# Gate and queries of the attention branch as seven block products, with GpSimd adding the token sums, in a one-core hybrid retention and differential-attention step

## What is computed

```python
h = rmsnorm(x, norm1_g) * (1.0 + scale1) + shift1
proj = h @ w_in
q_r, k_r, v_r, g_r, q_d, k_d, v_d, gates = split_projection(proj)
gates = jax.nn.sigmoid(gates + b_gate)
gate_r, gate_d = jnp.split(gates, 2, axis=-1)
...  # rotary positions on q_r, k_r, q_d, k_d of the latent tokens
y_r = head_group_norm(out_f + jnp.flip(out_b_rev, 1), ret_gn_g)
branch_r = (jax.nn.silu(g_r) * y_r) @ w_ret_out
...  # differential attention of q_d over k_d, v_d and the cached keys and values
mix = (gate_r * branch_r + gate_d * branch_d) @ w_o
x = x + gate1 * mix
ffn = (jax.nn.silu(h2 @ w_ffn_gate) * (h2 @ w_ffn_up)) @ w_ffn_down
```

## Time and profile before

| | us |
|---|---|
| median of three runs | 1299.69 |
| lowest, highest | 1299.42, 1299.79 |
| the profiled execution | 1299.46 |
| its span, first to last instruction | 1297.8 |

### The profile page before, as it was taken

How to read it: one execution, slowest core, us unless ns; L and a number is a source line. 1 busy time by engine, 2 the same in 40 slices (tenths; PEclk the granted TensorE clock), 3 DMA queues, 4 the chain that set the end, 5 groups by cost and what they waited for, 6 DMA issues and landing times.

```text
span 1297.8 us, 19779 instructions
## 1 busy us (share of the span) xinstructions
PE 1259.1 (97%) x7734; PEld 1152.0 (89%) x7734; DVE 798.2 (62%) x1297; ACT 486.7 (38%) x813; POOL 300.7 (23%) x264
## 2 busy tenths in 40 slices
PE   4999999999999999999999999989999999999997
PEld 2698888899999999988788899889998999889986
DVE  4654121477657743374798844478973789557966
ACT  5452233344321122223777622245441344313434
POOL 1002000311000111110799400004510445005500
PEclk9999999999999999999999999999999999999999
DMA  9634222154434434451200234311333133222222
GB/s 309 210 98 138 65 65 82 41 157 136 129 132 130 146 98 130 114 178 50 82 2 1 82 98 146 93 38 33 98 98 97 33 97 99 97 65 66 90 89 81
DMA packets 87394, 129.59 MB, mean 100 GB/s; under 512 B 3529, under 2 KB 64450, under 8 KB 87186
## 3 DMA queue, kind: packets, MB, share of 16 engines
q1 hardware_dynamic: 77024, 95.69, 23.1%
q0 software_dynamic: 8960, 31.68, 8.1%
q10 hardware_dynamic: 1330, 1.10, 0.3%
HBM read 117.43 MB, written 4.73 MB: 94 GB/s over the span
## 4 chain that ended last, share of the span: by engine, by line
PE 90%; DVE 4%; ACT 3%; POOL 1%; issue 1%; DMA 1%; ACTq 0%; DVEq 0%
PE psum L431 31%; PE psum L468 28%; PE psum L687 18%; PE psum L1240 2%; PE psum L1224 1%; PE psum L417 1%; PE psum L1199 1%; PE psum L617 1%; PE psum L1049 1%; POOL probs L989 1%; DVE w_lo L400 1%; DMA rows<-in_diff_subln_g 1%; PE psum L1157 1%; PE psum L1197 1%; POOL probs L995 1%
## 5 line engine op out<-in xcount | busy, mean ns | idle before, releaser
L400 DVE TENSOR_TENSOR w_lo<-w_raw,w_hi 128x2048 fp32r<-128x2048 f32 x57 | 130.6, 2291 | 191.6 <-ACT w_hi L395 189.2
L395 ACT ACTIVATE w_hi<-w_raw 128x2048 fp32r<-128x2048 f32 x57 | 108.8, 1909 | 173.9 <-PE psum L468 107.8
L431 PE MATMUL psum<-h_hi,w_lo 128*128 128x320 f32 x672 | 154.7, 311 | 0.0
L431 PE MATMUL psum<-h_lo,w_hi 128*128 128x320 f32 x672 | 153.1, 309 | 0.0
L431 PE MATMUL psum<-h_hi,w_hi 128*128 128x320 f32 x672 | 153.1, 309 | 0.0
L468 PE MATMUL psum<-w_hi,hid 128*128 128x512 f32 x440 | 135.6, 389 | 0.0
L431 PEld LDWEIGHTS psum<-h_hi,w_hi 128*128 128x128 f32 x672 | 112.4, 188 | 0.0
L431 PEld LDWEIGHTS psum<-h_hi,w_lo 128*128 128x128 f32 x672 | 111.8, 188 | 0.5 <-issue 0.4
L431 PEld LDWEIGHTS psum<-h_lo,w_hi 128*128 128x128 f32 x672 | 112.2, 188 | 0.0
L687 PE MATMUL psum<-h_hi,seven_lo 128*128 128x320 f32 x320 | 98.9, 309 | 1.1 <-DVE silu_g L2296 1.1
L687 PE MATMUL psum<-h_lo,seven_hi 128*128 128x320 f32 x320 | 98.9, 309 | 0.0
(11 more groups left out here) (311 smaller groups left out, 2754.7 us busy)
## 6 DMA issues: line engine op xcount, KB each, us to landing
w_raw<-in_w_in SPq DMA_DIRECT2D x32, 1024.0 KB, 5.6
ada_b<-in_w_ada POOLq DMA_DIRECT2D x32, 512.0 KB, 4.4
w_raw<-in_w_ffn_gate SPq DMA_DIRECT2D x11, 1024.0 KB, 5.3
w_raw<-in_w_ffn_up SPq DMA_DIRECT2D x11, 1024.0 KB, 5.3
ada_a<-in_w_ada SPq DMA_DIRECT2D x8, 1024.0 KB, 13.6
w_raw<-in_w_ffn_down SPq DMA_DIRECT2D x8, 1024.0 KB, 5.1
w_raw<-in_w_ret_out SPq DMA_DIRECT2D x4, 1024.0 KB, 5.2
swapped<-qk_d POOLq DMA_DIRECT2D x32, 128.0 KB, 2.5
```

The costliest lines, as they stand in the source:

```text
L395: act.activation(w_hi[s][:, :, :], w_raw[s][:, :, :], ACT.Copy).then_inc(w_hi_done, 1)
L400: dve.tensor_tensor(w_lo[s][:, :, :], w_raw[s][:, :, :], w_hi[s][:, :, :].bitcast(F32), ALU.subtract).then_inc(w_lo_done, 1)
L431: last = pe.matmul(bank(4 * par + 2 * j + h, HALF), w[:, k, cs], x[:, k, h * HALF:(h + 1) * HALF], start=(k == 0 and n == 0), stop=(k == K ...
```

## The change

- gate_d and q_d are made by seven products of blocks, like the up phases, eight units in all; both are read out by VectorE. The order becomes gate_r, ret_out, gate_d, q_d.
- ret_out comes ahead of gate_d: the transposes of retention's output are woven into gate_r's third unit, and all four heads are normalised and gated ahead of that.
- The token block sums of h, out of high and low parts, are made by GpSimd in ten operations of 128x1280, two behind the loads of gate_r's last and each ret_out partial; ScalarE and VectorE split them.
- VectorE adds the seven products of a query unit, ScalarE scales them in place, and the rotation of unit n-1 stands in VectorE's program inside unit n of the seven units, that of (1,0) ahead of the split of the first key unit, that of (1,1) behind it.
- The adaLN partials that stood beside gate_d stand beside k_d, with buffers of their own; v_d's first stands in k_d's last rotation.
- Addresses move (gate_d, qk_d, od, v_d, the rotary table); the rows of gate1 and gate2 are loaded by two DMAs.

The diff, cut to its core (`seven_sums` is the five steps of `seven_unit`, moved to a function that both use, with the two places between them as arguments; `weight_sums` keeps its four sums, the fourth now apart as `last_weight_sum`; `B`, `Y` and so on are places in SBUF):

```diff
 PHASES = [("qk_r", 4, "act", "act"), ("v_r", 4, "act", "act"), ("g_r", 4, "act", "act"),
-          ("gate_r", 4, "act", "act"), ("gate_d", 4, "act", "act"), ("ret_out", 4, "dve", "dve"),
-          ("q_d", 4, "act", "act"), ("k_d", 4, "act", "act"), ("v_d", 4, "act", "act"),
+          ("gate_r", 4, "act", "act"), ("ret_out", 4, "dve", "dve"), ("gate_d", 4, "dve", "dve"),
+          ("q_d", 4, "dve", "dve"), ("k_d", 4, "act", "act"), ("v_d", 4, "act", "act"),
           ("diff_out", 4, "dve", "dve"), ("w_o", 4, "dve", "dve"),
...
-ADA_FIRST = {"gate_r": 0, "gate_d": 4, "ret_out": 8, "v_d": 12}
+ADA_FIRST = {"gate_r": 0, "ret_out": 4, "k_d": 8, "v_d": 12}
+SEVENS = ("gate_d", "q_d", "up0", "up1", "up2")
+GATED = ("gate_d", "q_d")
...
+        h_sum_hi = [at(f"h_sum_hi{n}", B + 5 * n, [P, KH, HALF], F32R) for n in range(4)]
+        h_sum_lo = [at(f"h_sum_lo{n}", Y + 5 * n, [P, KH, HALF], F32R) for n in range(4)]
+        h_sum = [at(f"h_sum{n}", Y + 5 * n, [P, KH, HALF]) for n in range(4)]
...
+            def token_terms():
+                hi, lo = (h_hi[:, :, :].bitcast(F32), h_lo[:, :, :].bitcast(F32))
+                x11, x21, x12, x22 = (hi[:, ks, cs] for ks in (low_k, high_k) for cs in (first_half, second_half))
+                y11, y21, y12, y22 = (lo[:, ks, cs] for ks in (low_k, high_k) for cs in (first_half, second_half))
+                z = [t[:, :, :] for t in h_sum]
+                return ((z[0], x21, x22, ALU.add), (z[0], z[0], y21, ALU.add), (z[0], z[0], y22, ALU.add),
+                        (z[1], z[0], x11, ALU.subtract), (z[1], z[1], y11, ALU.subtract),
+                        (z[3], x12, z[1], ALU.subtract), (z[3], z[3], y12, ALU.add),
+                        (z[2], x11, x21, ALU.subtract), (z[2], z[2], y11, ALU.add), (z[2], z[2], y21, ALU.subtract))
+            terms = token_terms()
+            def add_token_terms(first, end):
+                for n in range(first, end):
+                    out, x, y, op = terms[n]
+                    pool.wait_ge(h_sum_step, n) if n else pool.wait_ge(n2t["yg"]["ps"], KT)
+                    pool.tensor_tensor(out, x, y, op).then_inc(h_sum_step, 1)
+            with pool.Fori(0, 2) as i:
+                for par in range(2):
+                    load_ada("gate_r", i, par)
+            add_token_terms(0, 2)
+            for i in range(2):
+                for par in range(2):
+                    load_ada("ret_out", i, par)
+                    add_token_terms(2 + 4 * i + 2 * par, 4 + 4 * i + 2 * par)
+            def turn_queries(i, par):
+                swap_halves("q_d", qk_d, P // 4, 4, 0, i, par, swapped_d)
+            for n, unit in enumerate(gated_units):
+                if n == 1:
+                    pool.wait_ge(ada_step, 16 * 9)
+                    pool.dma_start(rope_d[:, :, :], a["const_rope_diff"].rearrange("a p t -> p a t")).then_inc(ld_rope, 16)
+                weight_sums(*unit)
+                if n >= 6:
+                    turn_queries(*gated_units[n - 2][1:])
+                last_weight_sum(*unit)
+            turn_queries(1, 0)
+            pool.wait_ge(mm_done, ready("q_d", 1, 1, 1))
+            load_ada("k_d", 0, 0)
+            turn_queries(1, 1)
+            following = [("k_d", 0, 1), ("k_d", 1, 0), ("k_d", 1, 1), ("v_d", 0, 0)]
+            for n, (i, par) in enumerate(((0, 0), (0, 1), (1, 0), (1, 1))):
+                load_ada(*following[n])
+                swap_halves("k_d", qk_d, P // 4, 8, DH, i, par, swapped_d)
+            pool.wait_ge(rope_done, 12 + AHEAD)
...
-            pe_dense(pe, "gate_r", pe_T_unit, h_hi, h_lo, first=1)
             pe.wait_ge(y_gated, RH)
-            pe_T_and_dense(pe, "yg", y_nat, "gate_d", h_hi, h_lo)
+            pe_T_and_dense(pe, "yg", y_nat, "gate_r", h_hi, h_lo, i=1)
             pe_dense(pe, "ret_out", pe_T_unit, yg_hi, yg_lo)
-            pe_dense(pe, "q_d", pe_T_unit, h_hi, h_lo)
+            for unit in gated_units:
+                pe_seven(pe, *unit)
             pe_dense(pe, "k_d", pe_T_unit, h_hi, h_lo)
...
+            def high_of_h_sum(place):
+                n, terms = ((0, 3), (1, 5), (3, 7), (2, 10))[place]
+                act.wait_ge(h_sum_step, terms)
+                act.activation(h_sum_hi[n][:, :, :], h_sum[n][:, :, :], ACT.Copy).then_inc(x_sum_h, 1)
+            def finish_gated(name, i, par):
+                act.wait_ge(freed["dve"], freed_after(name, i, par, 1))
+                tile = 4 * i + 2 * par
+                if name == "q_d":
+                    both = qk_d[:, tile:tile + 2, :]
+                    act.activation(both, both, ACT.Copy, scale=DHD ** -0.5).then_inc(q_scaled, 1)
+                    return
+                for j in range(2):
+                    act.activation(gate_d[:, tile + j, :], gate_d[:, tile + j, :], ACT.Sigmoid,
...
+            for h in range(RH):
+                normalize_head(h)
+            gate_of_retention(0, 0)
+            act_split(act, unit_of("gate_r", 0, 1) + 1, 0)
+            gate_of_retention(0, 1)
             act_to_T(act, "yg", yg_hi, gn_gain)
-            dense("gate_d", gate("gate_d", gate_d, KT))
-            dense("ret_out", lambda i, par: None)
-            dense("q_d", copy_T("q_d", qk_d, 0, DHD ** -0.5))
+            for par in range(2):
+                act_split(act, unit_of("gate_r", 1, par) + 1, 1 - par)
+                gate_of_retention(1, par)
+            act_split(act, unit_of("ret_out", 0, 0) + 1, 1)
+            act_split(act, unit_of("ret_out", 0, 1) + 1, 0)
+            high_of_h_sum(0)
+            act_split(act, unit_of("ret_out", 1, 0) + 1, 1)
+            for place in range(1, 4):
+                high_of_h_sum(place)
+            prefill("gate_d", (B11, B21, T1, B22), ready("ret_out", 1, 0, 1))
+            prefill("gate_d", (T2, T4, T3), ready("ret_out", 1, 1, 1))
+            previous = None
+            for n, unit in enumerate(gated_units):
+                following = gated_units[n + 1] if n + 1 < len(gated_units) else None
+                if following:
+                    act_seven(act, *following, B11)
+                copy_first(*unit)
+                if previous:
+                    finish_gated(*previous)
+                if following:
+                    for p in (B21, T1, B22, T2, T4, T3):
+                        act_seven(act, *following, p)
+                else:
+                    act.wait_ge(seven_mm, (SEVEN - 1) * seven_index(*unit) + B22 + 1)
+                    act_split(act, unit_of("k_d", 0, 0), 0)
+                previous = unit
+            finish_gated(*previous)
             dense("k_d", copy_T("k_d", qk_d, DH, 1.0))
...
+            dve_split(dve, unit_of("gate_r", 0, 0) + 1, 1)
+            ada_partial("gate_r", 0, 0)
+            for h in range(RH):
+                gate_head(h)
+            dve_split(dve, unit_of("gate_r", 0, 1) + 1, 0)
+            ada_partial("gate_r", 0, 1)
+            ada_partial("gate_r", 1, 0, range(KT // 2))
             dve_to_T(dve, "yg", yg_hi, yg_lo, gn_gain)
-            for i in range(2):
-                for par in range(2):
-                    dve_split(dve, unit_of("gate_d", i, par) + 1, 1 - par)
-                    ada_partial("gate_d", i, par, range(0 if i or par else KT // 2, KT))
+            for par in range(2):
+                dve_split(dve, unit_of("gate_r", 1, par) + 1, 1 - par)
+                ada_partial("gate_r", 1, par, range(0 if par else KT // 2, KT))
...
+            def low_of_h_sum(place):
+                n, terms = ((0, 4), (1, 6), (3, 7), (2, 10))[place]
+                dve.wait_ge(x_sum_h, place + 1)
+                dve.wait_ge(h_sum_step, terms)
+                dve.tensor_tensor(h_sum_lo[n][:, :, :], h_sum[n][:, :, :], h_sum_hi[n][:, :, :].bitcast(F32), ALU.subtract).then_inc(x_sum_l, 1)
...
-            dense("ret_out", gated_ret)
-            ada_partial("v_d", 0, 0)
+            first = gated_units[0]
+            dve_split(dve, unit_of("ret_out", 0, 0) + 1, 1)
+            ada_partial("ret_out", 0, 0)
+            gated_ret(0, 0)
+            dve_split(dve, unit_of("ret_out", 0, 1) + 1, 0)
+            ada_partial("ret_out", 0, 1)
+            low_of_h_sum(0)
+            gated_ret(0, 1)
+            dve_split(dve, unit_of("ret_out", 1, 0) + 1, 1)
+            ada_partial("ret_out", 1, 0)
+            low_of_h_sum(1)
+            gated_ret(1, 0)
+            weights_low(first, (B11, B21))
+            ada_partial("ret_out", 1, 1)
+            for place in (2, 3):
+                low_of_h_sum(place)
+            weights_low(first, (T1, B22))
+            gated_ret(1, 1)
+            weights_low(first, (T2, T4, T3))
...
+            def gated_unit(n):
+                name, i, par = gated_units[n]
+                following = gated_units[n + 1] if n + 1 < len(gated_units) else None
+                tile = 4 * i + 2 * par
+                out = (gate_d if name == "gate_d" else qk_d)[:, tile:tile + 2, :]
+                def after_first():
+                    if following:
```

(29 more changed lines are left out.)

346 lines of the change are left out of this document (192 added, 154 removed).

## The result

The changed kernel takes 1306.08 us (median of 5 runs, 1305.16 to 1307.50), the kernel before 1299.69 (5 runs, 1299.42 to 1300.33): ratio 1.0049, 95% interval 1.0036 to 1.0063. The prediction said 1299.5 with a range to 1305.0; it was 6.6 us too fast. In the profiled executions the span went from 1297.8 to 1304.3, by 6.5 us.

What follows compares the result with a forecast made beforehand. TensorE, busy for 97% of the span, was taken as the bound. 13.9 us gained against 0.6 + 0.2 + 2.35 + 3.3 + 2.2 + 5.1 = 13.75 lost gave 1299.5 us; 8-in-10 range 1293.5 to 1305.

Steps and rivals of the forecast that it cites:

- The gain of 13.9: TensorE in gate_d and q_d: eight units go from 14.09 to 12.36 us each, 13.9 us gained.
- Token sums at 2.9: GpSimd's ten token sums of 1280 elements take 2.9 us each, the middle of 2.6 and 3.15.
- That they block the partials: GpSimd's sums shut out VectorE's adaLN partials in gate_r's last and ret_out's units; TensorE waits 0.2 us, at ret_out(1,0).
- partials that keep 0.40 us a step beside GpSimd: Sign that the forecast is wrong: adaLN partials not slowed by GpSimd; the time would then be near 1293.7.
- rival (a): The sums cost little: 2.6 us terms that don't block partials, smaller waits; 1293.7 us, with milder mixes down from 1297.1; chance 0.28.
- ret_out(1,1), 2.35: Retention's last output unit: its partial queues behind low parts of B11 and B21, held by GpSimd's tenth term; TensorE waits 2.35 us.
- First seven unit, 3.3: gate_d(0,0): VectorE's owed token low parts and turns of GpSimd's weight sums make TensorE wait 3.3 us.
- Unit 6, 2.2: Queries' rotation delays unit 5's last sum to about +8.5 of unit 6, whose T2 needs the shared tile: 2.2 us wait.
- rival (c): VectorE bounds the query units: 1305.8 or 1303.6 us; sign: over three waits above 1 us, gate_d(0,1) to k_d; chance 0.25.
- Unit 7, none: Last query unit: no wait, as GpSimd has no weight sums left and unit 6's late end gives room.
- First key unit, 5.1: k_d's first product: split stands behind the rotation of (1,0), whose swapped halves come late; TensorE waits 5.1 us (4.0 to 5.2).
- Keys and values covered: Key and value units: VectorE's 12.1 us per key unit fits in 14.97; tightest cover 1.3 at v_d(0,1)'s split; cost nothing.

Runs made afterwards that it cites:

- e6_terms_mid: The changed kernel with GpSimd's two token sums of each retention-output unit put between the two loads of w_ada: 1304.88 us, one run.
- e2_load_later: The changed kernel with SyncE's w_in loads for k_d(0,0) and k_d(0,1) held until the swapped halves of q_d(0,1) and q_d(1,0) landed: 1299.46 us.
- e1_split_first: The changed kernel with the split for k_d(0,0) put ahead of the rotation of (1,0) in the last query unit: 1304.60 us.
- e3_both: The changed kernel with both the earlier split for k_d(0,0) and the two w_in loads held for the swapped halves: 1302.71 us.
- e5_terms_first: The changed kernel with GpSimd's two token sums of each retention-output unit put ahead of the loads of w_ada: 1309.21 us.
- e11_short_sums: The changed kernel with work left out: six of the ten token sums made over 32 elements only, four whole: 1301.62 us.

## Why the prediction was wrong, step by step

- **The gain of 13.9**: right. 12.37 us for 84 products, where 12.36 was forecast.
- **Token sums at 2.9**: right as a length (2.96 to 2.99 alone). *That they block the partials*: the exclusion is there, but in the changed kernel a sum met only the first step of two partials (3.05 and 3.06 us instead of 0.34) or the split, and the cover of the units took it. 0.2 forecast, 0 measured. One of the signs of being wrong, partials that keep 0.40 us a step beside GpSimd, came true in e6_terms_mid, and the time was not near rival (a) for it: the partials' term was too small to matter.
- **ret_out(1,1), 2.35**: right in mechanism, 1.9 in size. Doing the partial first removed the wait, and so did shorter sums.
- **First seven unit, 3.3**: right in mechanism (short sums removed it), 2.4 in size, of which 1.6 show as low clock that hid waits: where the clock stayed up, 1.4 to 2.4 us of waits stood in its place.
- **Unit 6, 2.2**: right place and releaser chain, 1.5. The 2.2 did not follow from its own rows: 5.8 + 2.2 of rotation is 8.0 and not 8.5, and 8.0 less 6.56 is 1.5. VectorE's last sum in fact ended 8.05 us into unit 6. GpSimd's turns did stretch the rotation there (steps of 2.2 to 2.3 us instead of 1.22), which is what rival (c) said, but in this unit alone.
- **Unit 7, none**: wrong, by the same transfers as the next term. VectorE waited 2.08 us for the swapped halves, and TensorE 1.6 in turn; with the loads held back there was no wait.
- **First key unit, 5.1**: this is the step that failed. Its order was read rightly (the split behind the waiting rotation), and with an undisturbed transfer it measured 4.6. Its term "four issues and the landing take 4.4 us" came from the earlier trace rows, where the transfer had the DMA engines almost to itself: in the kernel before, a weight load is released by the split, and the split stands behind the rotation, so the load (471.8 to 477.3) was nearly through when the halves were issued (476.4). In a seven unit the load is released by the low part of T3, early in the next unit. The load for k_d(0,1) starts at 488.6 and the swap at 489.2, and the 128 KB pieces then land after 6.9 to 7.75 us. I had counted the issue and the landing of the moved step's own transfers, not what else would be under way when they are issued. The collision itself could have been read in the kernel before, in the queries of retention: the swap in two pieces of 256 KB is issued at 75.0 and 75.6, SyncE's next load starts at 75.5, and one piece lands after 3.2 us, the other after 7.5.

```profile
L928 POOL DMA_DIRECT2D swapped<-qk_r x2: 605/609/613, 75.0 to 75.6; - x2
DMA to landing us min/median/max: 3.2/5.3/7.5
...
75.50 43.85 SPq L852 DMA_DIRECT2D w_raw<-in_w_in  x4
```

- **The clock**: not in the sum at all. The waits of the key units, and what the column sums and the 96 products after them lost: 4.6 and 1.6 us (e2_load_later), 5.8 and 3.4 (e1_split_first), 6.7 and 3.6 (e3_both), 9.9 and 2.9 (the changed kernel); behind 0.3 us, 0.2. The loss does not go by the length of the wait: three other runs with 9.8 to 10.0 us there lost 1.9 (e5_terms_first), 1.8 (e6_terms_mid) and 2.4 (e11_short_sums). A forecast wait of 5.1 should have carried 1.6 or more.
- **Keys and values covered**: right in the changed kernel (units 14.97 apart).
- **Rival (c)** named a time near the result (1303.6 to 1305.8) for a reason that held in unit 6 alone: in unit 7 and ahead of the keys VectorE stood idle for 8.1 us, waiting for transfers. Its sign, more than three waits over 1 us between gate_d(0,1) and k_d, did not come: there were two.

Still open: what decides which side waits when a run of scalar_tensor_tensor and a GpSimd operation meet, and why the 1.9 us wait in ret_out(1,1) was followed by a low clock in some kernels (0.89 in 389 to 404 in the changed one) and not in others (1.00 in 385 to 400 in e1_split_first, the same wait).

## What to carry to other kernels

When a change moves the instruction that frees a buffer, it moves the load that this buffer waits for: list what each load's release stood behind before, and which small, urgent transfer it can now run into. If a small transfer feeds the queue on which everything waits, let the large load wait for it; here two such waits, on one queue, were worth 6.6 us. A wait removed by reordering one engine has to be followed down the other engines' queues too, or it reappears one unit later (5.8, 6.7 and 3.8 us in three of these runs), and a wait of 4 us or more on TensorE should be priced with the slow products that follow it (1.6 to 3.6 us here).

## What the runs showed of the hardware

- Four transfers of 128 KB, the first issued 0.5 to 0.9 us behind the start of a 1 MB load, landed after 6.0 to 7.75 us instead of 2.2 to 2.7; the load itself took 7.0 to 8.8 us, against 5.5 in the kernel before. The four are issued from GpSimd and the load from SyncE, and that kept nothing apart: the Trainium skill (DMA: Bandwidth & Descriptors, "Issuing engines are not separate DMA queues") says that transfers of all issuing engines run on the same DMA engines and interleave, and this case's rows agree. With three megabytes started together the one wanted first took 9.9.
- A tensor_scalar with one tensor in SBUF and one column waited for a GpSimd sum of 2.97 us (0.34 us became 3.12).
- A GpSimd sum issued inside a run of fourteen scalar_tensor_tensor waited 2 us for its end, and did not slow them; elsewhere single steps of such a run, begun 0.1 us after a GpSimd weight sum had, took 1.52 us instead of 0.47.
- TensorE's granted clock fell to 0.50 during a wait of 9.9 us and stayed there for about 6 us of the products behind it. Waits of 3.8 to 10.0 us cost 1.6 to 3.6 us in this way, in no order by length; the same 3.8 us wait cost 1.7 us in one run and 2.6 in the next.
